# Gated MLPs: the second products by Strassen's scheme, seven block products for eight, with the weight sums on GpSimd

## The reference

```python
def conv_ffn(xn, w_up, conv_w, conv_b, w_down):
    """Gated MLP; causal depthwise conv (width 3) on the gate branch before SiLU."""
    seq = xn.shape[1]
    val, gate = jnp.split(xn @ w_up, 2, axis=-1)
    gp = jnp.pad(gate, ((0, 0), (CONV_W - 1, 0), (0, 0)))
    gc = conv_b + conv_w[0] * gp[:, 0:seq]
    for j in range(1, CONV_W):
        gc = gc + conv_w[j] * gp[:, j:j + seq]
    return (jax.nn.silu(gc) * val) @ w_down
...
        h = h + conv_ffn(rms_norm(h, ffn_norm[layer]), ffn_w_up[layer], ffn_conv_w[layer],
                         ffn_conv_b[layer], ffn_w_down[layer])
```

## Time and profile before

| what | value |
|---|---|
| runs: median (lowest to highest) | 1983.34 us (1982.88 to 1983.55) |
| span of the profiled execution, first to last instruction | 1981.3 us |
| what lies around it in the median of the runs | 2.0 us |
| PE busy in the span | 1953.9 us, 99%, 9474 matmuls |
| PE weight loads busy | 1562.3 us, 79% |
| DVE, ACT, POOL busy | 1329.3 (67%), 900.1 (45%), 243.7 us (12%) |
| DMA, mean over the span | 91 GB/s |

### The profile page before, as it was taken

The page is one execution under the profiler, slowest core; times in us unless marked ns, Lnnn a source line. Parts: engine busy times, 40 slices in busy tenths (PEclk is TensorE's granted clock), DMA queues, the critical chain, the costliest instruction groups (busy, mean ns, idle before and its releaser), DMA issues.

```text
span 1981.3 us, 25092 instructions
## 1 busy us (share of the span) xinstructions
PE 1953.9 (99%) x9474; PEld 1562.3 (79%) x9474; DVE 1329.3 (67%) x1907; ACT 900.1 (45%) x1483; POOL 243.7 (12%) x237
## 2 busy tenths in 40 slices
PE   9999999999999999999999999999999999999998
PEld 7777888888888776788888888788888888886666
DVE  8995476446644449747644664778787778437985
ACT  5674332223233348733222223565555545236774
POOL 4131100000010000010000001133333332000002
PEclk9999999999999999999999999999999999999998
DMA  8465322232233220022223223222222223322112
GB/s 290 113 144 155 106 83 92 88 121 91 81 105 106 86 96 11 1 90 91 93 88 117 96 77 107 86 64 70 86 75 80 85 65 107 96 75 75 38 38 75
DMA packets 81367, 180.44 MB, mean 91 GB/s; under 512 B 17888, under 2 KB 33632, under 8 KB 81248
## 3 DMA queue, kind: packets, MB, share of 16 engines
q1 hardware_dynamic: 77680, 172.08, 27.9%
q0 software_dynamic: 3424, 6.23, 1.1%
q10 hardware_dynamic: 144, 0.52, 0.1%
HBM read 171.53 MB, written 7.27 MB: 90 GB/s over the span
## 4 chain that ended last, share of the span: by engine, by line
PE 85%; DVE 8%; ACT 3%; issue 2%; DMA 1%; SPq 1%; POOLq 0%; POOL 0%; DVEq 0%; ACTq 0%
PE psum L431 20%; PE psum L434 20%; PE psum L432 20%; PE psum L472 2%; PE psum L473 2%; PE psum L475 2%; PE psum L453 2%; PE psum L899 1%; PE psum L901 1%; PE psum L900 1%; PE psum L1781 1%; PE psum L456 1%; PE psum L454 1%; PE psum L2824 1%; DVE wl L402 1%
## 5 line engine op out<-in xcount | busy, mean ns | idle before, releaser
L402 DVE TENSOR_TENSOR wl<-raw,wh 128x1024 fp32r<-128x1024 f32 (+3 forms) x337 | 381.4, 1133 | 303.6 <-ACT wh L391 302.9
L431 PE MATMUL psum<-xh,wh 128*128 128x512 f32 x1376 | 543.9, 395 | 1.7 <-DVE xl L550 1.7
L434 PE MATMUL psum<-xh,wl 128*128 128x512 f32 x1376 | 537.0, 390 | 1.6 <-DVE wl L402 1.6
L432 PE MATMUL psum<-xl,wh 128*128 128x512 f32 x1376 | 536.4, 390 | 0.0
L391 ACT ACTIVATE wh<-raw 128x1024 fp32r<-128x1024 f32 (+3 forms) x337 | 316.0, 939 | 294.8 <-PE psum L434 198.1
L431 PEld LDWEIGHTS psum<-xh,wh 128*128 128x128 f32 x1376 | 258.6, 188 | 61.9 <-issue 2.9
L434 PEld LDWEIGHTS psum<-xh,wl 128*128 128x128 f32 x1376 | 258.7, 188 | 57.9 <-DVE wl L402 3.7
L432 PEld LDWEIGHTS psum<-xl,wh 128*128 128x128 f32 x1376 | 258.8, 188 | 55.1 <-issue 2.4
L577 POOL TENSOR_TENSOR rs<-rs,sq 128x512 f32<-128x512 f32 x35 | 46.6, 1331 | 1088.8 <-ACT sq L562 1088.8
L434 PE MATMUL psum<-fh,wl 128*128 128x512 f32 x352 | 136.9, 389 | 0.0
L432 PE MATMUL psum<-fl,wh 128*128 128x512 f32 x352 | 136.9, 389 | 0.0
(11 more groups left out here) (526 smaller groups left out, 3339.1 us busy)
## 6 DMA issues: line engine op xcount, KB each, us to landing
raw<-d_w SPq DMA_DIRECT2D x224, 512.0 KB, 3.5
raw<-d_w SPq DMA_DIRECT2D x32, 384.0 KB, 3.0
raw<-d_w SPq DMA_DIRECT2D x48, 256.0 KB, 2.6
raw<-d_w SPq DMA_DIRECT2D x32, 320.0 KB, 2.9
Mt<-d_kd SPq DMA_DIRECT2D x64, 64.0 KB, 2.4
bc<-d_bc SPq DMA_DIRECT2D x8, 256.0 KB, 5.3
d_ud<-ust SPq DMA_DIRECT2D x8, 256.0 KB, 3.1
U<-d_ud POOLq DMA_DIRECT2D x64, 32.0 KB, 2.4
```

What stands on the lines that cost most here:

```text
L402: dve.e.tensor_tensor(K.wl[n % NH][:, 0:COLS[n]], K.raw[n % RAW][:, 0:COLS[n]], K.wh[n % NH][:, 0:COLS[n]].bitcast(F32), ALU.subtract).the ...
L431: pe.e.matmul(b[:, :], WH[:, o:o + P], XH, start=(k == k0), stop=False)
L432: pe.e.matmul(b[:, :], WH[:, o:o + P], XL, start=False, stop=False)
L434: mm = pe.e.matmul(b[:, :], WL[:, o:o + P], XH, start=False, stop=(k == k1 - 1))
```

## The change

The down product of each layer is made in blocks of two by two. For a pair q of output tiles (4 pairs) and a pair k of hidden tiles, and with the tokens halved (256 left, 256 right), a 2 x 2 block matrix of weights meets a 2 x 2 block matrix of hidden values. The eight block products are replaced by seven, by Strassen's scheme in Winograd's form: seven weight forms (A11, A12, A22 and the sums S1 to S4), seven hidden forms (B11, B21, B22 and T1 to T4), and sums behind the products.

- Units: 44 units of kind "S" for each layer (4 pairs q by 11 pairs k) replace 32 units of kind "T". Each is loaded as 512 columns. POOL makes S1 to S4 from them in the same `raw` buffer (`weight_sums`: an add of 128 x 256 and two of 128 x 128, each after the one before), and ACT and DVE then split 896 columns. `split_hi` of such a unit waits for POOL (`wsum`) in the place of the DMA.
- PE: 21 matmuls of 256 columns for each unit, into four banks for each pair q.
- The hidden tiles: halves of 12 and 10 tiles in the place of 11 and 11. DVE makes T1 to T4 in four adds of 128 x 256, ACT and DVE split 1792 columns for a pair of tiles in the place of 1024 (`hidden_dve`).
- Behind the products of a pair q: ACT copies 256 columns out of a bank, and DVE does eight adds (`seven_to_h`: three of 512 columns, five of 256) in the place of two of 512.
- Splits, norms and squares are placed anew: the norm of two tiles stands behind a pair q, and POOL does the sums of the pairs 0 to 2, then the squares 1 to 3, then the sums of pair 3, then the squares 4 to 7.
- Elsewhere only names of semaphores and one choice of a spare buffer in the attention stage change.

```diff
-            for m in range(8):
-                tile(f"down{i}", m, half * HALF, (half + 1) * HALF)
+            for q in range(DOWN_PAIRS):
+                for k in range(f0, f1, 2):
+                    u.append((f"down{i}", "S", q, k, k + 2))
...
+def weight_sums(K, pool, n0, n1):
...
+        pool.wait_ge(f"raw{n % RAW}", 16 * (n // RAW + 1))
+        pool.e.tensor_tensor(s13.rearrange("p (n c) -> p n c", n=2), a21.unsqueeze(1).broadcast_to([P, 2, P]),
+                             others.rearrange("p (n c) -> p n c", n=2), ALU.add).then_inc(K.S["pool"], pool.up())
+        pool.wait_ge("pool", pool.n)
+        pool.e.tensor_tensor(s2, s1, a11, ALU.add).then_inc(K.S["pool"], pool.up())
+        pool.wait_ge("pool", pool.n)
+        pool.e.tensor_tensor(s4, s2, a12, ALU.add).then_inc(K.S["wsum"], 1)
...
+    for k in range(k0, k1, 2):
+        n, WH, WL = next_unit(K, pe, name, "S", q, k)
+        pe.wait_ge("hi", n + 1)
+        begun = set()
+        for form, block, bank, side in SEVEN:
+            out = K.bank[banks[bank]][:, 256 * side:256 * side + 256]
+            o = form * P
+            XH, XL = x(k, block)
+            first = k == k0 and bank not in begun
+            begun.add(bank)
+            pe.e.matmul(out, WH[:, o:o + P], XH, start=first, stop=False, skip_group_check=True)
+            pe.e.matmul(out, WH[:, o:o + P], XL, start=False, stop=False, skip_group_check=True)
+            pe.wait_ge("lo", n + 1)
+            mm = pe.e.matmul(out, WL[:, o:o + P], XH, start=False, stop=(k == k1 - 2), skip_group_check=True)
+        mm.then_inc(K.S["unit"], 1)
...
+    split_lo(K, dve, end + 1 + LA)
+    dve.wait_ge(*before)
+    dve.wait_ge("unit", end)
+    a = add(h1, h1, p23[:, :], ALU.add)
+    dve.wait_ge("fa", copy)
+    u = add(U, p16[:, R], p1, ALU.subtract)
+    dve.wait_ge("dve", a)
+    add(h1[:, L], h1[:, L], p1, ALU.add)
+    dve.wait_ge("dve", u)
+    w = add(Q, U, p7[:, L], ALU.subtract)
+    if not last:
+        split_lo(K, dve, end + 2 + LA)
+    b = add(h1[:, R], h1[:, R], U, ALU.subtract)
+    c = add(h2, h2, p45[:, :], ALU.add)
+    dve.wait_ge("dve", b)
+    e.tensor_tensor(h1[:, R], h1[:, R], p45[:, R], ALU.subtract).then_inc(K.S[signal], 1)
+    dve.wait_ge("dve", max(w, c))
+    two = h2.rearrange("p (n c) -> p n c", n=2)
+    e.tensor_tensor(two, two, Q.unsqueeze(1).broadcast_to([P, 2, 256]), ALU.add).then_inc(K.S[signal], 1)
...
+        for q in range(DOWN_PAIRS):
+            for k in range(f0, f1, 2):
+                split_hi(K, act, UNIT[(down, "S", q, k)] + 1 + LA)
+            end = pair_done(down, q, f1)
+            split_hi(K, act, end + 1 + LA)
+            act.wait_ge("unit", end)
...
+            act.e.activation(K.T[:, 512:768], K.bank[DOWN_BANKS[half][q % 2][0]][:, 0:256], ACT.Copy).then_inc(K.S["fa"], 1)
+            if half == 0 or q < 3:
+                split_hi(K, act, end + 2 + LA)
+            if half:
+                norm_act(K, act, b + 1, 2 * q)
+                norm_act(K, act, b + 1, 2 * q + 1)
...
+def hidden_dve(K, dve, layer, half, f):
...
+    e.tensor_tensor(T2, t[:, R], T1, ALU.subtract).then_inc(K.S["dve"], dve.up())
+    e.tensor_tensor(T3, t[:, R], before[:, R], ALU.subtract).then_inc(K.S["dve"], dve.up())
+    dve.wait_ge("dve", dve.n)
+    e.tensor_tensor(T4, t[:, L], T2, ALU.subtract).then_inc(K.S["gv"], 1)
+    for first, n, count, src in (("B21", 2, g + 2, t[:, :]), ("T1", 4, g + 3, K.T[:, :])):
+        dve.wait_ge("fh", count)
+        e.tensor_tensor(hidden(K.fl[layer], half, f, first, n), src, hidden(K.fh[layer], half, f, first, n).bitcast(F32),
+                        ALU.subtract).then_inc(K.S["fl"], 1)
...
 def ffn_pool(K, pool, layer):
-    add_squares(K, pool, 2 + 2 * layer)
+    down, (f0, f1), b = f"down{layer}", SPANS[1], 2 + 2 * layer
+    weight_sums(K, pool, UNIT[(down, "S", 0, 0)], pair_done(down, 2, f1))
+    add_squares(K, pool, b, 1, 4)
+    weight_sums(K, pool, UNIT[(down, "S", 3, f0)], pair_done(down, 3, f1))
+    add_squares(K, pool, b, 4, 8)
```

More of the change, by code:

```diff
@@ L307, with pair_done @@
 OFFS = [P * sum(COLS[:n]) for n in range(len(UNITS) + 1)]
+SUMS = [sum(u[1] == "S" for u in UNITS[:n + 1]) for n in range(len(UNITS))]
+SPLIT = [(P, 7 * P) if u[1] == "S" else (0, c) for u, c in zip(UNITS, COLS)]
 def done(name, m, k0=0, k1=8):
     return UNIT[(name, "T", m, pieces(k0, k1)[-1][0])] + 1
+def pair_done(name, q, k1):
+    return UNIT[(name, "S", q, k1 - 2)] + 1
 SEMS = (
@@ new lines, with seven_products @@
+A22, A11, A12, S1, S3, S2, S4 = range(7)
+SEVEN = ((A11, "B11", 0, 0), (A12, "B21", 2, 0), (S4, "B22", 2, 1), (A22, "T4", 3, 0), (S1, "T1", 3, 1), (S2, "T2", 0, 1),
+         (S3, "T3", 1, 0))
+def seven_products(K, pe, name, q, banks, x, freed, k0, k1):
+    for b in banks:
+        take(pe, b, freed)
+    for k in range(k0, k1, 2):
[13 more added lines that the diff above has]
+        mm.then_inc(K.S["unit"], 1)
@@ new lines, in seven_to_h, with add @@
+def seven_to_h(K, dve, q, banks, end, copy, before, signal, last):
+    h1, h2, e = K.h[:, 2 * q, :], K.h[:, 2 * q + 1, :], dve.e
+    U, Q, p1 = K.T[:, 0:256], K.T[:, 256:512], K.T[:, 512:768]
+    L, R = slice(0, 256), slice(256, 512)
+    p16, p7, p23, p45 = (K.bank[b] for b in banks)
+    def add(out, x, y, op):
+        e.tensor_tensor(out, x, y, op).then_inc(K.S["dve"], dve.up())
+        return dve.n
+    split_lo(K, dve, end + 1 + LA)
[17 more added lines that the diff above has]
+    e.tensor_tensor(two, two, Q.unsqueeze(1).broadcast_to([P, 2, 256]), ALU.add).then_inc(K.S[signal], 1)
@@ L569, in norm_act, with add_squares @@
     square_h(K, act, b, k)
[L572 to L574 removed]
+def add_squares(K, pool, b, k0=1, k1=8):
+    for k in range(k0, k1):
         pool.wait_ge("sq", 8 * b + k + 1)
@@ L763, in ffn_act @@
     rsqrt_first(K, act, b)
-    for half in range(2):
-        for f in range(half * HALF, (half + 1) * HALF):
+    for half, (f0, f1) in enumerate(SPANS):
+        for f in range(f0, f1):
             i = layer * NF + f
@@ L770, in ffn_act @@
             act.other("silu")
-            act.e.activation(t[:, :], t[:, :], ACT.Silu).then_inc(K.S["silu"], 1)
+            act.e.activation(t[:, :], t[:, :], ACT.Silu).then_inc(K.S["fa"], 1)
             split_hi(K, act, v + 1 + LA)
[L773 to L778, removed]
-            if half:
-                norm_act(K, act, b + 1, m)
+            if half:
+                act.wait_ge("unit", pair_done(down, 3, SPANS[0][1]))
```

152 lines of the change are left out of this document (102 added, 50 removed).

## The result

The changed kernel takes 2005.11 us (median; 2002.38 to 2005.9) beside 1983.44 us for the kernel before on the same chip: a ratio of 1.0105, 95% interval 1.0091 to 1.012, so slower by 21.7 us. The forecast was 1989.5 us, its range 1972 to 2006. The direction holds, and the range by 0.9 us only; the stretch 1981 to 1997, to which the forecast gave 51%, was missed. The sum has 6.2 of the 21.7 us.

A forecast was written before the change was run, and what follows sets the result against it. TensorE, busy 1953.9 of 1981.3 us, bounds the kernel; per layer -8.8 (shorter stream) +2.2 (turns) +9.7 (pair ends) = +3.1 us, +6.2 for both: span 1987.5, with 2.0 around it 1989.5 us, range 1972 to 2006.

The forecast's parts named there:

- The sum: Whole kernel: TensorE's gain of 8.8 us against turns 2.2 and pair ends 9.7, +3.1 us a layer, +6.2 for both.
- TensorE's gain: Down products: 924 matmuls a layer at 0.120 us, 110.9 us in place of 119.6, a gain of 8.8 us a layer.
- What a unit costs the others: Down units: GpSimd adds of 0.74 and 0.46 us, 2.6 us a unit with VectorE's sharing, against TensorE's 2.52.
- the lead of three units: First-half down products: five raw buffers let GpSimd run about 6 us ahead, covering the 1.7 us that 24 units fall behind.
- The ends of pairs, second half: Second-half down products: holes of 1.8, 2.5, 1.1 (start of pair 3) and 4.3 us, 9.7 us a layer.
- The turn: From up to down products: the third unit's low part comes late, 1.1 us a turn, 2.2 us a layer.
- 80% hides as long as its waits for ScalarE between stay under a fifth. I book nothing: Up products: about 2.4 us more VectorE adds a pair of tiles hide under TensorE's 21.8 us, costing nothing.
- The waits for SBUF do not add up: Faster rival: GpSimd's adds slip between VectorE's, holes only 3.7 us a layer, -10 us, 1973 us; chance 30%.
- GpSimd becomes the bound: Slower rival: small adds a fifth dearer, about 3.0 us a unit in down products, +18 us on the forecast, 2007; chance 16%.

The follow-up runs named there:

- run 12: Changed kernel with pair-end splits ahead of norms, VectorE's gate multiply ahead of its weight split, and copies loaded in place of GpSimd's sums (another output): 1966.83 us.
- run 4: Seven products in the first halves only, second halves as in the kernel before, whose up products use banks 5 to 7 to avoid bank waits: 1985.47 us.
- run 1: Changed kernel without GpSimd's weight sums, each unit loaded as seven blocks with copies of A21 where sums stood, so another output: 1983.89 us.
- run 2: Changed kernel with the split of each pair's last unit ahead of the norms, on ScalarE and VectorE in the second halves: 1994.64 us.
- run 8: Changed kernel with second-half pair-end splits ahead of the norms and GpSimd's sums of pair 3's first two units ahead of squares 1 to 3: 1994.4 us.
- run 7: Changed kernel with two VectorE lines swapped in the up products, so the gate's multiply by the root goes ahead of the weight split: 1993.78 us.
- run 6: Changed kernel with the first convolution step of each gate tile moved from VectorE to ScalarE: 2020.8 us.
- run 5: Changed kernel with 18 useless 256-column matmuls added at the largest hole of each first turn and of each pair 3: 1999.45 us.
- run 10: Changed kernel with second-half pair-end splits ahead of the norms and VectorE's gate multiply ahead of its weight split in the up products: 1983.77 us.
- run 11: Changed kernel with pair-end splits ahead of norms, VectorE's gate multiply ahead of its split, and pair 3's first unit's sums ahead of squares 1 to 3: 1982.62 us.

## Why the prediction was right, and where not

**The number: luck in part.** 2005.11 us lies in the range, 0.9 us below its end. That end was set for small adds of GpSimd nearly a fifth dearer, which they were not; what took the time there were two other things, the first turns and the clock. The direction is no luck: the ends of pairs alone make 9.1 us of holes a layer beside the 8.8 gained, near to what was booked.

**TensorE's gain: right.** 0.120 us a start, and 16.5 us in run 12 against 17.6. The Trainium skill, page "TensorE: Matmul & The Clock Gate", section "Back-to-back issue gap", gives 262 cycles for 256 columns, an estimate of 109 ns at 2.4 GHz; the page calls this the gap of an isolated matmul. The stream of this trace, each matmul with its own weight load, is at 120.

**What a unit costs the others: right.** 0.74 and 0.46 us for undisturbed adds, 2.51 us a unit beside VectorE in pair 3. The first halves keep up but for the turn, as the lead of three units said (run 4).

**The ends of pairs, second half: right in place and size.** Booked 1.8, 2.5, 1.1 and 4.3 us; measured 1.3, 2.4, 1.2 and 4.2: 9.1 for 9.7 a layer. Run 1 splits it: the norms ahead of the split make 3.5 us a layer without any sum, and the sums the rest; run 2 shows that the place of the split is what decides at the pairs' ends, and its wait at the start of pair 3 points to GpSimd's squares, which run 8 confirms (3.6 us became 1.3 with two units' sums ahead of them).

**The turn: the step that failed.** "I book 1.1 us for each turn" holds for the second turns (1.3 each) and not for the first (4.4 and 3.9). It was worked out as if VectorE came to the turn level with TensorE, and that rests on "80% hides as long as its waits for ScalarE between stay under a fifth. I book nothing". The up products themselves kept up (what TensorE waits there for low parts went from 1.6 to 2.4 us in the whole kernel), so nothing was booked for a good reason; but VectorE starts each gated MLP several us late, behind the norm's root, and 21.3 us of work and waits in TensorE's 21.8 leave 0.5 us a pair of tiles to catch up. The lag at 302.61 us is 4.8 us and at 377.13 still 3.2. In the kernel before the cycle of 9.82 us a tile against 10.88 had removed it after six tiles:

```profile
269.31 0.68 DVE L705 TENSOR_TENSOR fg<-psum,rs 128x512 f32<-128x512 f32 x1
279.13 0.68 DVE L705 TENSOR_TENSOR fg<-psum,rs 128x512 f32<-128x512 f32 x1
...
329.46 0.69 DVE L705 TENSOR_TENSOR fg<-psum,rs 128x512 f32<-128x512 f32 x1 [0.96 <-PE psum L434]
```

(A lag is the distance from the end of a gate tile's last matmul to VectorE's first step on it.) Run 7 (lag gone, turn 1.4), run 6 (lag kept, 3.5 to 5.6 at all turns) and the second half of the changed kernel (0.1 us of lag at the turn, hole 1.3) show the cause from three sides. GpSimd has a share in it too: without its sums the lag at the turn is 2.0 us in the place of 3.2, and layer 0's first turn costs 2.8 us (run 1) in the place of 4.4; with the swap it costs 1.4, and with the swap and no sums 0.35 (run 12). So most of the 4.4 is the lag, and some 1 to 1.6 the sums, for which 0.2 was booked. The error is 6.1 us of holes.

**The clock: missing from the sum.** Holes were priced at their length. Behind the larger ones TensorE ran at 1.2 GHz for 3.41 or 6.83 us, 7.8 us in all; run 5 shows it. The two errors make 13.9 us; the second turns add 0.4 and the ends of pairs take 1.2: 13.1 of the 16.6 us between the forecast span of 1987.5 and the measured one. The rest is the 3.5 us above.

**The rivals.** "The waits for SBUF do not add up" fell by its own measure: it decided at 6.8 us of holes a layer, and 14.6 were measured. With the sums, run 10 takes 16.9 us more than run 12, and the changed kernel 21.2 more than run 1; how much of that is waits for SBUF was not separated. "GpSimd becomes the bound" came to 2007, which is near the time, but is not the cause: its adds cost what the forecast said, the first halves keep up (run 4), and the holes that could be traced to a late sum stand where pair 3 starts, where its squares are ahead of its sums. That a number is hit by another road is luck. What would have made the prediction wrong by its own text (gapless second halves, holes in up phases, holes in each unit) did not happen, but for the 0.8 us more of waits in up products.

**What stays open.** Why the half clock lasts 3.41 us in one place and 6.83 in another was not found. Nor was a placement of the squares that serves pair 3 and the next norm alike: run 11 still has holes of 0.5 to 1.5 us in pairs 2 and 3. What of the 17 us of the sums is VectorE's sharing and what is lateness of the sums themselves was not separated. The runs without sums also load 448 KB a unit in the place of 256 and start ScalarE's split by the DMA, so they change more than the adds. Holes and half clock were counted in one profiled execution of each kernel. The swap of two lines was not tried in the kernel before, whose TensorE has no hole at that place.

## What to carry to other kernels

An engine's load in a stretch says whether it keeps up, not where it stands when the stretch ends: write down its cycle with the waits inside it, the lag with which it comes in, and how many cycles it has to lose it. A wait inside an in-order queue is as good as work: moving 0.55 us of work to another engine for a wait of 0.95 lost 15.7 us, and letting a step pass a wait that it does not need gained 11.3. And price holes in TensorE's stream with the clock behind them: here groups of holes of 3.9 to 4.4 us were followed by half clock that cost some 1.5 to 2.4 us more.

## What the runs showed of the hardware

A stream of 256-column matmuls starts one each 0.120 us at 2.4 GHz and 0.213 at 1.2 GHz. After TensorE's holes of 4.4 us at the first turn (381.9 to 389.1 us) and of 4.2 us in pair 3 the clock was 0.50 for 3.41 or 6.83 us; after holes of 0.56 and 1.84 us at the end of pair 1 (593.4 and 595.6 us) it stayed at 1.00, while in run 7 it fell behind 0.27 and 1.84 us at the same place (at 590.2 us). With no hole over 1.7 us (run 11) it never fell between 5 and 1971 us; holes of 1.63 and 1.08 us at layer 1's first turn in run 1 were followed by half clock, and 1.69 and 1.08 us in layer 0 were not. VectorE's in-order queue, which had 0.55 us of elementwise work on 512 columns taken from it by ScalarE (0.82 us there), stood still for 0.95 (run 6).
